# The end of the second layer: a product that sums and spreads the squares, and the power taken over 128x256 elements

## The chip, the cores and the metric

The kernel runs on one core of one Trainium2 chip. The metric is the device time of one execution in microseconds, lower is better. Engines go by their short names: PE is TensorE (PEld its weight loads), DVE is VectorE, ACT is ScalarE, POOL is GpSimd, SP is SyncE, which only issues transfers here.

## The reference

Everything is float32: the model width D is 1024, the inner width E is 2048, the sequence S is 512, and there are two layers. Only the last line below is touched by the change.

```python
def _rmsnorm(x, g):
    y = x * lax.rsqrt(jnp.mean(x * x, axis=-1, keepdims=True) + EPS)
    return y * g

for i in range(2):
    shift, scale, gate = _modulation(c, w_mod[i], b_mod[i])
    h = _rmsnorm(x, norm_g[i]) * (1.0 + scale) + shift
    y = _short_conv_mixer(h, ...) if i == 0 else _spatial_gating_mixer(h, ...)
    x = x + gate * y
return _rmsnorm(x, final_g)
```

## The kernel before

The residual `x` lies transposed in SBUF: 128 partitions hold the 128 features of one tile, KD = 8 tiles lie one behind the other (`x_b[:, k, :]`), and the 512 positions of the sequence run along the free dimension. So the mean over the features that the norm needs is a sum over the eight tiles and then over the 128 partitions, and its reciprocal root, one number for each position, must be on all partitions before it can be multiplied into `x`.

Every large product is computed in three parts (high times high, high times low, low times high) by float32r operands. In the second layer's output projection, `out_product` makes six of the eight feature tiles (three rounds of two) over all 512 positions; `last_out_product` makes the last two tiles in two halves of 256 positions (`halves[0]`, `halves[1]`), so that the norm of the first half can be made while PE computes the second.

After each pair of tiles DVE adds the gated product to `x` (`update_x`, `update_half`), ACT squares the new tiles (`square_x`, `square_half`), and DVE adds the squares into `ssum` (`add_squares`, L1446). The very last square is not added; it stays in `work[:, 1, HALF:S]` and PE adds it. For each half the order around the change is:

1. PE, `half_sums`: two products with one block of 128 columns of `ssum` as weights and one column of ones as the moving operand (L1000), and two more with the last square (L1004). The sums land with the positions on the partitions, 128x2.
2. DVE, `start_rstd` (L1450): scale and EPS, PSUM to `variance`, 128x2. It raises `var_ready`.
3. POOL (L519): `variance` to the power of -0.5 into `rstd`, all 128x4 elements. It raises `power_ready`.
4. DVE, `diagonals` (L1456): two 128x128 diagonal matrices out of the identity and `rstd`.
5. PE, `broadcast` (L1010): a matrix of ones times the diagonals, 128x256, so that every partition has the row of the 256 values.
6. DVE (L2104): for each of the 8 tiles `x = x * final_g * p_half`, reading the values from PSUM. After each two of them SP sends 128x2x256 elements out (L496).

Each engine does its instructions in the order in which they are written, and semaphores are the only order between engines. DVE's order at the end is: `update_half(1, 0)`, steps 2, 4 and 6 of the first half, then `update_half(1, 1)`, steps 2, 4 and 6 of the second. PE's order is: the two last tiles of the first half; the first round (s = 0) of the second half; `half_sums(1, 0)`; the round s = 1; `broadcast`; the rounds s = 2 and 3; then `half_sums(1, 1)`, `keep_clock(8)` (eight 128x128 products of ones, L979, whose result nobody reads) and the second `broadcast`. POOL takes six powers in all (`N_RSQRT`); numbers 5 and 6 are those of the two halves. The first layer's end and the start use the same functions and stay as they are.

Of the kernel before, what the change touches and what calls it, by code (L numbers as in the profile page):

```python
# [31 lines left out]
ALU = mybir.AluOpType  # L32

P = 128
D = 1024
S = 512
E = 2048
KD = D // P
KE = E // P
NCH = S // P  # L40
HALF = S // 2
EPS = 1e-6
# [3 lines left out]
N_RSQRT = 6  # L46
X_STEPS = KD + 2 + 1
SQUARES = KD + 2
SQ_STEPS = 1 + 6 + 2
SQ_START = 7  # L50
FREE = 2
WARM = (6, 2)
WARM_END = 8
LEAD = 0
AHEAD = 3
OFF = 6
# [81 lines left out]
def build(nc, stream, xt, cols_d, wst_d, bs_d, out):  # L138
    ctx = ExitStack()
    with ctx:  # L140
# [10 lines left out]
        def at_kb(name, kb, shape, dt=F32):  # L151
            return nc.alloc_sbuf_tensor_at(name, shape, dt, offset=base + 1024 * kb)
# [44 lines left out]
        raw = at_kb("raw", 156, [P, RING, SLOT])  # L197
        tmp = at_kb("tmp", 176, [P, 4, S])
        work = at_kb("work", 184, [P, 2, S])
        ssum = at_kb("ssum", 196, [P, S])  # L200

        cols = sb("cols", [P, N_COL])
# [3 lines left out]
        variance = sb("variance", [P, NCH])  # L206
        rstd = sb("rstd", [P, NCH])
# [4 lines left out]
        minus_half = sb("minus_half", [P, NCH])  # L212
        ones = sb("ones", [P, P])
# [30 lines left out]
        sq_ready = sem("sq_ready")  # L244
# [4 lines left out]
        sq_added = sem("sq_added")  # L249
        stat_sum, var_ready, power_ready = sem("stat_sum"), sem("var_ready"), sem("power_ready")  # L250
        half_done = sem("half_done")
        diag_ready, rstd_bc = sem("diag_ready"), sem("rstd_bc")
# [56 lines left out]
        halves = [slice(0, HALF), slice(HALF, S)]  # L309
# [45 lines left out]
        p_half = [p_rstd, p_pair[0]]  # L355
# [144 lines left out]
        @block.gpsimd  # L500
        def _(pool):
            pool.memset(ident[:, :], 0.0).then_inc(consts, 1)
            pool.memset(ones[:, :], 1.0).then_inc(consts, 1)
            pool.wait_ge(consts, 2)
            pool.affine_select(out=ident[:, :], in_=ident[:, :], compare_op=ALU.not_equal, fill=1.0, base=0,
                               pattern=[[-1, P]], channel_multiplier=1).then_inc(consts, 1)
            pool.memset(minus_half[:, :], -0.5).then_inc(consts, 1)
            pool.wait_ge(consts, 4)
            def low_b(i, g):
                pool.wait_ge(neg_b, of_b(i, g, 1, 1))  # L510
                pool.sem_inc(lo_begun_b, 1)
                pool.dma_start(wl_b[g][:, B_2:B_11].bitcast(F32), raw[:, 2 * g + 1, :],
                               accum_op=ALU.add).then_inc(b2_in_b[g], 16)

            for k in range(N_RSQRT):
                if k == 3:
                    low_b(0, 0)
                pool.wait_ge(var_ready, k + 1)
                pool.tensor_tensor(rstd[:, :], variance[:, :], minus_half[:, :], ALU.pow).then_inc(power_ready, 1)  # L519
                if k == 0:  # L520
                    for n, w in enumerate(BY_DMA):
                        slot = w_at(w)[0]
                        pool.wait_ge(neg_w, n + 1)
                        pool.dma_start(w_lo_s[:, w % 4, :].bitcast(F32), raw[:, slot, :],
                                       accum_op=ALU.add).then_inc(w_lo_in[slot], 16)
                    with pool.Fori(1, PAIRS) as i:
                        for g in range(4):
                            par = g % 2
                            pool.wait_ge(neg, of_pair(i, g, 1, 1))
                            pool.sem_inc(lo_begun, 1)  # L530
                            pool.dma_start(wl[par][:, B_2:B_11].bitcast(F32), raw[:, 2 * par + 1, :],
                                           accum_op=ALU.add).then_inc(b2_in[par], 16)
                    pool.wait_ge(y_made, PAIRS)
                if k == 3:
                    with pool.Fori(0, PAIRS - 1) as i:
                        low_b(i, 1)
                        low_b(i + 1, 0)
                    low_b(PAIRS - 1, 1)
                    pool.wait_ge(sv_used, 2 + KE)
                if k in (0, 3):  # L540
                    pool.wait_ge(stat_sum, 1 if k == 0 else 3)
                    pool.memset(ssum[:, :], 0.0).then_inc(sq_added, 1)
# [410 lines left out]
        def _(pe):  # L953
# [22 lines left out]
            def keep_clock(n):  # L976

                for _ in range(n):
                    pe.matmul(pp[3][:, 0:P], ones[:, :], ones[:, :], start=True, stop=True)  # L979
# [16 lines left out]
            def half_sums(layer, half):  # L996

                pe.wait_ge(sq_added, SQ_START + SQ_STEPS * layer + 1 + 6 + half + 1)
                for st in range(2):
                    pe.matmul(p_half[half][:, st:st + 1], ssum[:, HALF * half + P * st:HALF * half + P * (st + 1)],  # L1000
                              ones[:, 0:1], start=st == 0, stop=False, skip_group_check=True)
                pe.wait_ge(sq_ready, KD + SQUARES * layer + 6 + 2 * half + 2)
                for st in range(2):
                    mm = pe.matmul(p_half[half][:, st:st + 1], work[:, 1, HALF + P * st:HALF + P * (st + 1)],  # L1004
                                   ones[:, 0:1], start=False, stop=True, skip_group_check=True)
                mm.then_inc(stat_sum, 1)

            def broadcast(out, n, at):
                pe.wait_ge(diag_ready, n)
                pe.matmul(out, ones[:, :], work[:, 0, at], start=True, stop=True).then_inc(rstd_bc, 1)  # L1010
# [36 lines left out]
            for kp in range(4):  # L1047
# [8 lines left out]
                for n in range(2):  # L1056
                    k = 2 * kp + n
# [15 lines left out]
                for u in range(2):  # L1073
                    for n in range(2):
                        k = 2 * kp + n
                        at = slice(256 * (k % 4) + P * u, 256 * (k % 4) + P * (u + 1))
# [116 lines left out]
            def last_out_product(layer, w0):  # L1193

                for half in range(2):
                    for s in range(4):
                        out_slot(layer, w0, DPAIRS - 1, s)
                        for u in range(2):
                            if s == 0 and half == 1:
                                pe.wait_ge(x_updated, X_STEPS * layer + FREE + 6 + u)  # L1200
                            mm = unit(pp[last_bank(layer, half) + u][:, 0:HALF], weights(s, u, out_ring[layer]), rows(y_hi, halves[half]),
                                      rows(y_lo, halves[half]), range(4 * s, 4 * s + 4), s == 0, s == 3)
                            if half == 1:
                                mm.then_inc(blocks, 1)
                            elif s == 3:
                                mm.then_inc(half_done, 1)
                            if half == 1 and s == 0 and u == 1:
                                half_sums(layer, 0)
                            if half == 1 and s == 1 and u == 1:
                                broadcast(p_half[0][:, 0:HALF], 2 * layer + 3, slice(0, HALF))  # L1210


# [6 lines left out]
            for n in range(2):  # L1219
                mm = pe.matmul(p_pair[n].rearrange("q (h p) -> q h p", p=P), ones[:, :], ws[:, 4 * n:4 * n + 4, :],  # L1220
                               start=True, stop=True)
# [110 lines left out]
                out_product(1, W_BOUT, j)  # L1332
            pe.wait_ge(c_sum_b, OFF + 3 * 2 * PAIRS)
            last_out_product(1, W_BOUT)
            half_sums(1, 1)
            keep_clock(WARM_END)
            broadcast(p_half[1][:, 0:HALF], 6, slice(HALF, S))


        @block.vector  # L1340
        def _(dve):
# [5 lines left out]
            at = [0]  # L1347
# [104 lines left out]
            def diagonals(k, n, first):  # L1452

                dve.wait_ge(power_ready, k)
                for st in range(n):
                    ins = dve.tensor_scalar(work[:, 0, P * (first + st):P * (first + st + 1)], ident[:, :],  # L1456
                                            rstd[:, st:st + 1], None, ALU.mult)
                    if st < n - 1:
                        step(ins)
                ins.then_inc(diag_ready, 1)  # L1460
# [334 lines left out]
            def start_rstd(k, half):  # L1795
                dve.wait_ge(stat_sum, k if k < 4 else k - 1)
                rsqrt(k, p_half[half][:, 0:2], 1.0 / D, 2)
# [298 lines left out]

            for half in range(2):
                update_half(1, half)
                start_rstd(5 + half, half)
                diagonals(5 + half, 2, 2 * half)  # L2100
                dve.wait_ge(rstd_bc, 4 + half)
                for k in range(KD):
                    xa = x_b[:, k, halves[half]]
                    dve.scalar_tensor_tensor(out=xa, in0=xa, scalar=cols[:, C_FG + k:C_FG + k + 1],  # L2104
                                             in1=p_half[half][:, 0:HALF], op0=ALU.mult,
                                             op1=ALU.mult).then_inc(out_ready, 1)


# [74 lines left out]
```

## Time and profile before

| | us |
|---|---|
| median of 3 runs | 835.21 (833.79 to 835.49) |
| the profiled execution, its own time | 834.54 |
| its span in the trace | 832.4 |
| its mean granted PE clock | 0.994 of full speed |

The span runs from the first to the last record of the trace; the execution's own time has 2.1 us more around it. PE is busy for 97% of the span and POOL for 6%. Busy shares are those of the whole kernel; the change lies in the last 20 us, and only the records of that stretch tell what it does there. In the trace a float32 product appears as two records, so x4 is two products.

### The profile page before, as it was taken

Reading aid. Unit: us, or ns where it says so; the run is one execution under the profiler, and the core shown is the slowest. Engines: PE = TensorE matmul, PEld = TensorE weight load, DVE = VectorE, ACT = ScalarE, POOL = GpSimd, SP = SyncE. Lnnn points to the kernel's source line nnn. Section 1 sums busy time; section 2 is a strip of 40 time slices with the busy share of each in tenths; the row PEclk is TensorE's granted clock in tenths of the full one; section 3 lists DMA queues with packets and bytes.
Section 4 is the critical chain, followed back from the end, with each engine's and each line's share of the span. In section 5 each row is a group of like instructions: output and inputs, shape, how many; then the busy total and the mean of one; then the engine's idle time right before and its main releaser. Section 6 shows DMA issues by size and latency. Waiting matters only on the chain.

```text
span 832.4 us, 15163 instructions
## 1 busy us (share of the span) xinstructions
PE 804.5 (97%) x5590; PEld 750.3 (90%) x5590; DVE 643.7 (77%) x941; ACT 438.5 (53%) x617; POOL 52.1 (6%) x65
## 2 busy tenths in 40 slices
PE   5999999999999999999999999999999999899996
PEld 5779999999999999978889888899999999778896
DVE  5879999899998989887625776478888888676534
ACT  4575666666556565642225733356767666642210
POOL 1010000000100000000000000000000000000000
PEclk9999999999999999999999999999999999989999
DMA  9995565656566666497222342325445445574103
GB/s 353 364 245 140 142 201 169 208 166 189 176 184 177 197 168 198 135 378 258 96 77 77 142 162 101 101 77 152 124 128 148 135 145 151 181 299 152 51 1 102
DMA packets 39645, 138.36 MB, mean 166 GB/s; under 512 B 4288, under 2 KB 6464, under 8 KB 39616
## 3 DMA queue, kind: packets, MB, share of 16 engines
q1 hardware_dynamic: 32128, 111.16, 36.2%
q0 software_dynamic: 7056, 25.69, 16.2%
q10 hardware_dynamic: 432, 1.13, 0.3%
q8 instruction: 17, 0.28, 0.1%
q14 instruction: 12, 0.10, 0.0%
HBM read 108.09 MB, written 4.19 MB: 135 GB/s over the span
## 4 chain that ended last, share of the span: by engine, by line
PE 85%; issue 4%; ACT 4%; DVE 3%; DMA 2%; SPq 0%; POOL 0%; ACTq 0%; DVEq 0%; POOLq 0%
PE pp L1097 10%; PE pp L1098 10%; PE pp L1096 10%; PE pp L963 8%; PE pp L964 8%; PE pp L965 7%; PE p_aux L1096 6%; PE p_aux L1098 6%; PE p_aux L1097 6%; PE pp L1232 3%; PE pp L1234 3%; PE pp L1233 3%; PE pp L1053 2%; PE p_aux L1306 2%; DMA raw_s<-in_stream 1%
## 5 line engine op out<-in xcount | busy, mean ns | idle before, releaser
L1098 PE MATMUL pp<-h_hi,wl 128*128 128x256 f32 x280 | 79.2, 283 | 0.0
L1097 PE MATMUL pp<-h_lo,wh 128*128 128x256 f32 x280 | 79.2, 283 | 0.0
L1096 PE MATMUL pp<-h_hi,wh 128*128 128x256 f32 x280 | 79.2, 283 | 0.0
L1594 DVE TENSOR_TENSOR wl<-wt,wh 128x1024 fp32r<-128x1024 f32 x56 | 66.5, 1218 | 0.5 <-ACT wh L642 0.5
L642 ACT ACTIVATE wh<-wt 128x1024 fp32r<-128x1024 f32 x56 | 58.9, 1054 | 13.6 <-DVE wt L1575 7.6
L1096 PE MATMUL pp<-s_hi,wh 128*128 128x256 f32 x224 | 63.4, 283 | 0.0
L1097 PE MATMUL pp<-s_lo,wh 128*128 128x256 f32 x224 | 63.4, 283 | 0.0
L1098 PE MATMUL p_aux<-s_hi,wl 128*128 128x256 f32 x224 | 63.4, 283 | 0.0
L1098 PE MATMUL pp<-s_hi,wl 128*128 128x256 f32 x224 | 63.4, 283 | 0.0
L1097 PE MATMUL p_aux<-s_lo,wh 128*128 128x256 f32 x224 | 63.4, 283 | 0.0
L1096 PE MATMUL p_aux<-s_hi,wh 128*128 128x256 f32 x224 | 63.4, 283 | 0.0
L558 ACT ACTIVATE w_hi<-raw 128x1024 fp32r<-128x1024 f32 x29 | 30.6, 1058 | 62.0 <-PE pp L965 29.1
L963 PE MATMUL pp<-y_hi,w_hi_b 128*128 128x512 f32 (+1 forms) x160 | 57.9, 362 | 5.3 <-DVEq L2079 4.6
L963 PE MATMUL pp<-y_hi,w_hi 128*128 128x512 f32 (+1 forms) x160 | 58.5, 366 | 0.7 <-DVE y_lo L1655 0.3
L1371 DVE TENSOR_TENSOR w_lo<-raw,w_hi 128x1024 fp32r<-128x1024 f32 x32 | 38.9, 1222 | 23.1 <-ACT w_hi L558 22.4
L964 PE MATMUL pp<-y_lo,w_hi_b 128*128 128x512 f32 (+1 forms) x160 | 56.7, 354 | 0.0
L965 PE MATMUL pp<-y_hi,w_lo_b 128*128 128x512 f32 (+1 forms) x160 | 56.5, 353 | 0.0
L964 PE MATMUL pp<-y_lo,w_hi 128*128 128x512 f32 (+1 forms) x160 | 55.6, 348 | 0.0
L965 PE MATMUL pp<-y_hi,w_lo 128*128 128x512 f32 (+1 forms) x160 | 55.6, 347 | 0.0
L1097 PEld LDWEIGHTS pp<-h_lo,wh 128*128 128x128 f32 x280 | 53.8, 192 | 0.0
L1096 PEld LDWEIGHTS pp<-h_hi,wh 128*128 128x128 f32 x280 | 53.8, 192 | 0.0
L1098 PEld LDWEIGHTS pp<-h_hi,wl 128*128 128x128 f32 x280 | 53.8, 192 | 0.0
(223 smaller groups left out, 2584.2 us busy)
## 6 DMA issues: line engine op xcount, KB each, us to landing
raw<-in_stream SPq DMA_DIRECT2D x144, 512.0 KB, 4.0
wl<-raw POOLq DMA_DIRECT2D x28, 512.0 KB, 4.6
raw_l<-in_stream SPq DMA_DIRECT2D x18, 512.0 KB, 8.5
raw_s<-in_stream SPq DMA_DIRECT2D x16, 512.0 KB, 13.3
wl_b<-raw POOLq DMA_DIRECT2D x16, 512.0 KB, 4.5
raw_m<-in_stream SPq DMA_DIRECT2D x14, 512.0 KB, 3.2
w_lo_s<-raw POOLq DMA_DIRECT2D x5, 512.0 KB, 7.6
x_s<-in_xt SPq DMA_DIRECT2D x4, 512.0 KB, 5.9
```

The source lines that it names most:

```text
L558: act.activation(to[:, slot[0], :], raw[:, slot[1], :], ACT.Copy).then_inc(hi_cut, 1)
L642: act.activation(wh[g % 2][:, at], wt[g % 2][:, at], ACT.Copy).then_inc(t_hi_cut, 1)
L963: pe.matmul(out, hi, rhs_hi(kt), start=first and n == 0, stop=False)
L964: pe.matmul(out, hi, rhs_lo(kt), start=False, stop=False)
L965: mm = pe.matmul(out, lo, rhs_hi(kt), start=False, stop=last and n == len(kts) - 1)
L1096: pe.matmul(out, hi, hi_of(k), start=fresh and k == 0, stop=False, skip_group_check=not fresh)
L1097: pe.matmul(out, hi, lo_of(k), start=False, stop=False, skip_group_check=not fresh)
L1098: mm = pe.matmul(out, lo, hi_of(k), start=False, stop=k == 3, skip_group_check=not fresh)
L1232: pe.matmul(v_bank(st)[:, :], left_hi, right_hi, start=kt == 0, stop=False)
L1233: pe.matmul(v_bank(st)[:, :], left_hi, right_lo, start=False, stop=False)
L1371: dve.tensor_tensor(lo[:, slot[0], :], raw[:, slot[1], :], f32(hi[:, slot[0], :]), ALU.subtract).then_inc(consumed, 1)
L1594: dve.tensor_tensor(wl[par][:, part], wt[par][:, part], f32(wh[par][:, part]), ALU.subtract).then_inc(t_cut, 1)
```

## The change

In the second layer alone, `half_sums_wide` multiplies the matrix of ones by the 256 columns of `ssum` and then by those of the last square, into the same 128x256 block of PSUM. The sum is then on every partition at once. DVE turns it into `var_w` (128x256), POOL takes the power over 128x256 elements into `rstd_w` (the exponent is one column of `minus_half`, read 256 times), and the final multiplication reads `rstd_w` from SBUF. The diagonals, the broadcast and the eight clock keeping products are gone from this place. `var_w` and `rstd_w` lie where `work[:, 0, :]` and `tmp[:, 0, :]` are.

```diff
-WARM_END = 8
+        var_w, rstd_w = at_kb("var_w", 184, [P, S]), at_kb("rstd_w", 176, [P, S])
@@ gpsimd
                 pool.wait_ge(var_ready, k + 1)
-                pool.tensor_tensor(rstd[:, :], variance[:, :], minus_half[:, :], ALU.pow).then_inc(power_ready, 1)
+                if k < N_RSQRT - 2:
+                    pool.tensor_tensor(rstd[:, :], variance[:, :], minus_half[:, :], ALU.pow).then_inc(power_ready, 1)
+                else:
+                    at = halves[k - (N_RSQRT - 2)]
+                    pool.tensor_tensor(rstd_w[:, at], var_w[:, at], minus_half[:, 0:1].broadcast_to([P, HALF]),
+                                       ALU.pow).then_inc(power_ready, 1)
@@ tensor
+            def half_sums_wide(half):
+                out = p_half[half][:, 0:HALF]
+                pe.wait_ge(sq_added, SQ_START + SQ_STEPS + 1 + 6 + half + 1)
+                pe.matmul(out, ones[:, :], ssum[:, halves[half]], start=True, stop=False)
+                pe.wait_ge(sq_ready, KD + SQUARES + 6 + 2 * half + 2)
+                pe.matmul(out, ones[:, :], work[:, 1, HALF:S], start=False, stop=True).then_inc(stat_sum, 1)
@@ last_out_product
                             if half == 1 and s == 0 and u == 1:
-                                half_sums(layer, 0)
-                            if half == 1 and s == 1 and u == 1:
+                                if layer:
+                                    half_sums_wide(0)
+                                else:
+                                    half_sums(layer, 0)
+                            if half == 1 and s == 1 and u == 1 and not layer:
                                 broadcast(p_half[0][:, 0:HALF], 2 * layer + 3, slice(0, HALF))
@@ end of tensor
-            half_sums(1, 1)
-            keep_clock(WARM_END)
-            broadcast(p_half[1][:, 0:HALF], 6, slice(HALF, S))
+            half_sums_wide(1)
@@ end of vector
                 update_half(1, half)
-                start_rstd(5 + half, half)
-                diagonals(5 + half, 2, 2 * half)
-                dve.wait_ge(rstd_bc, 4 + half)
+                dve.wait_ge(stat_sum, 4 + half)
+                dve.tensor_scalar(var_w[:, halves[half]], p_half[half][:, 0:HALF], 1.0 / D, EPS, ALU.mult,
+                                  ALU.add).then_inc(var_ready, 1)
+                dve.wait_ge(power_ready, 5 + half)
                 for k in range(KD):
                     xa = x_b[:, k, halves[half]]
                     dve.scalar_tensor_tensor(out=xa, in0=xa, scalar=cols[:, C_FG + k:C_FG + k + 1],
-                                             in1=p_half[half][:, 0:HALF], op0=ALU.mult,
+                                             in1=rstd_w[:, halves[half]], op0=ALU.mult,
                                              op1=ALU.mult).then_inc(out_ready, 1)
```

## Rows read from the trace of the kernel before

**Rows 1.** Busy time of each engine over the whole span, share, instructions.

```profile
PE 804.5 (97%) x5590; PEld 750.3 (90%) x5590; DVE 643.7 (77%) x941; ACT 438.5 (53%) x617; POOL 52.1 (6%) x65
```

**Rows 2.** Busy time by stretch, us and instructions, the last 8.5 us.

```profile
core 0: us, PE busy (x) PEld busy (x) DVE busy (x) ACT busy (x) POOL busy (x), PEclk, DMA share, GB/s
...
823.90:832.40 8.50, 2.56 (x19) 2.00 (x18) 3.87 (x11) 0.00 (x0) 1.01 (x1) 0.78 0.37 123
```

**Rows 3.** Chain of waits in order of time, last stretch: start us, us, what.

```profile
816.88 0.12 PE pp L963
...
822.31 0.49 DVE x_b L1786
...
822.83 0.42 ACT work L783
...
823.29 0.61 PE p_aux L1004 x4
823.90 1.89 PE pp L979 x16
825.79 0.68 PE p_aux L1010 x2
...
826.49 0.48 DVE x_b L2104
```

**Rows 4.** Instructions in order of time, first half of the columns: start us, us, engine, line.

```profile
812.16 0.50 PE L1000 MATMUL p_aux<-ones,ssum 128*128 128x1 f32 x4
...
812.97 0.36 PE L963 MATMUL pp<-y_hi,w_hi_b 128*128 128x256 f32 x1
...
813.39 1.04 POOL L519 TENSOR_TENSOR rstd<-variance,minus_half 128x4 f32<-128x4 f32 x1 [88.55 <-DVE variance L1450]
...
815.93 0.59 PE L1010 MATMUL p_aux<-work,ones 128*128 128x256 f32 x2
816.17 0.47 PE L963 MATMUL pp<-y_hi,w_hi_b 128*128 128x256 f32 x1
816.48 0.28 PE L964 MATMUL pp<-y_lo,w_hi_b 128*128 128x256 f32 x1
...
816.56 3.22 DVE L2104 SCALAR_TENSOR_TENSOR x_b<-x_b,cols,p_aux 128x256 f32<-128x256 f32 x8 [1.61 <-PE p_aux L1010]
```

**Rows 5.** Instructions in order of time, second half of the columns.

```profile
820.87 0.48 DVE L1786 SCALAR_TENSOR_TENSOR x_b<-pp,mod,x_b 128x256 f32<-128x256 f32 x1 [1.09 <-PE pp L965]
...
824.18 1.01 POOL L519 TENSOR_TENSOR rstd<-variance,minus_half 128x4 f32<-128x4 f32 x1 [9.75 <-DVE variance L1450]
```

**Rows 6.** Two powers of layer one and the vector engine beside them.

```profile
443.81 1.04 POOL L519 TENSOR_TENSOR rstd<-variance,minus_half 128x4 f32<-128x4 f32 x1 [86.37 <-DVE variance L1450]
...
443.92 1.23 DVE L1371 TENSOR_TENSOR w_lo<-raw,w_hi 128x1024 fp32r<-128x1024 f32 x1 [0.20 <-ACT w_hi L558]
...
459.06 1.21 DVE L1371 TENSOR_TENSOR w_lo<-raw,w_hi 128x1024 fp32r<-128x1024 f32 x1
...
459.22 1.92 POOL L519 TENSOR_TENSOR rstd<-variance,minus_half 128x4 f32<-128x4 f32 x1 [14.37 <-DVE variance L1450]
```

**Rows 7.** GpSimd's other instructions, its groups by line, then in order of time.

```profile
L542 POOL MEMSET ssum<- 128x512 f32 x2 | 1.1, 528 | 29.8 <-DVE y L1649 15.5 <-DVE work L2005 14.3
...
0.89 0.21 POOL L503 MEMSET ones<- 128x128 f32 x1
1.34 0.29 POOL L505 TENSOR_SCALAR_AFFINE_SELECT ident<-ident 128x128 f32<-128x128 f32 x1 [0.25 <-POOL ones L503]
1.58 0.10 POOL L507 MEMSET minus_half<- 128x4 f32 x1
```

**Rows 8.** Groups of vector instructions by line and shape: busy us, mean ns.

```profile
L1422 DVE SCALAR_TENSOR_TENSOR acc_b<-raw_l,silu_c,acc_b 128x256 f32<-128x256 f32 x42 | 20.4, 485 | 1.9
...
L1943 DVE TENSOR_TENSOR tmp<-pp,pc_b 128x256 f32<-128x256 f32 x16 | 6.7, 417 | 1.3 <-PE pp L1098 1.3
...
L2104 DVE SCALAR_TENSOR_TENSOR x_b<-x_b,cols,p_aux 128x256 f32<-128x256 f32 x16 | 6.4, 475 | 2.4 <-PE p_aux L1010 2.4
```

## The prediction, made before the changed kernel ran

> **What bounds the kernel now.** I read the busy shares first: PE works 97% of the span and POOL 6% [rows 1]. That says that no time is won by relieving POOL in general, but nothing of the end, since the change touches only the last 20 us. So the second view is the stretch from 823.90 us on: of 8.50 us PE is busy 2.56, DVE 3.87 and POOL 1.01 [rows 2]. No engine is full there; the end is a chain of short steps, each of which waits for the one ahead. The third view, the chain of waits, gives these steps in order [rows 3]: DVE adds the last tile (822.31), ACT squares it (822.83 to 823.25), PE sums (823.29 to 823.90), then the eight clock keeping products and the broadcast, and DVE begins to multiply at 826.49. In the chain 823.90 to 825.79 is booked on L979, but that is only what PE did meanwhile: the broadcast had to wait for POOL's power, 824.18 to 825.19 [rows 5], and for the diagonals behind it. From 826.49 to the end of the span at 832.4 are 5.91 us, which hold eight multiplications and the last transfer, and the change leaves them in kind.
>
> For the first half of the columns the same steps lie beside PE's products [rows 4]: DVE's eight multiplications run 816.56 to 819.78, and DVE then sits idle 1.09 us until PE frees it at 820.87 [rows 5]. That idle time is all the slack that the first half has.
>
> **The change part by part.**
>
> PE, first half. The narrow sums stop the stream from 812.16 to 812.97, 0.81 us [rows 4]. For the wide form the nearest row is the broadcast, a product of the same shape: the stream's products begin 0.12 us apart [rows 3], at the broadcast it is 815.93, 816.17, 816.48, so it costs 0.24 + 0.31 - 0.12 = 0.43 us [rows 4]. Two wide products cost 0.86, and the broadcast's 0.43 goes: PE gets to its last product 0.81 + 0.43 - 0.86 = 0.38 us earlier. If DVE is free, its last update then begins at 820.49 instead of 820.87.
>
> DVE. The 128x256 evacuation from PSUM replaces one of 128x2. The nearest row is L1943, 128x256 out of PSUM, 417 ns [rows 8]; I take 0.40 us. The diagonals go. The multiplications read their second operand from SBUF instead of PSUM: with all operands in SBUF L1422 takes 485 ns, with PSUM L2104 takes 475 [rows 8]. Eight times 10 ns is 0.08 at most, taken as nothing.
>
> POOL. This is the term that decides, and no row shows a power over more than four columns. Call its duration T. The record for 128x4 is 1.01 to 1.04 us [rows 4, 5], and it is not the price of a first call: the one at 824.18 is the next instruction that POOL computes after the one at 813.39, and is only 0.03 shorter. What is inside this microsecond? Two records tell. At 443.81 a large DVE instruction starts 0.11 us after the power and doesn't disturb it, 1.04 us. At 459.06 the same DVE instruction starts 0.16 us ahead of it, and the power takes 1.92: it ends at 461.14, which is 0.87 us after DVE's end at 460.27 [rows 6]. So POOL reads all its operands in about the first 0.1 us and is held when DVE is reading; the other 0.87 us is computing and writing of four columns. Against that, a memset of the same 128x4 is 0.10 us, one of 128x128 0.21 and one of 128x512 0.53 [rows 7]: moving a column costs (528 - 206) / 384 = 0.84 ns. The microsecond is therefore the power's own arithmetic, and the question is how much of it comes again with each column.
>
> Lower bound: none of it does, and each further column costs what a memset's does, T = 1.03 + 252 x 0.00084 = 1.24 us. Upper bound: all but the memset's 0.10 is proportional, T = 0.10 + 256 x 0.93 / 4 = 59.6 us. I take a value near the upper end, since the only row of a power is nearer to it: a fixed part of 0.34 us, the memset's 0.10 and the 0.24 that lies between the end of a memset's record (0.89 + 0.21) and the instruction that waits for it at 1.34 [rows 7], and 0.69 / 4 = 0.1725 us a column. T = 0.34 + 256 x 0.1725 = 44.5 us.
>
> A rule of the Trainium skill gives this a reason. GPSIMD Engine Reference, Performance pitfalls for Q7 kernels: a dependent chain of float32 operations costs 4 cycles for each of them unless independent work fills in. At the 1.2 GHz of its Specifications, 0.1725 us is 207 cycles, as an estimate some 52 dependent operations for a column. No row here shows whether columns overlap.
>
> The sum. First half: the wide sums end at 812.16 + 0.43 + 0.59 = 813.18; DVE takes 0.05 + 0.40; POOL starts 0.08 later, ends after T; DVE multiplies 0.04 behind it, at 813.75 + T, for 3.22 us. DVE is free at 817.0 + T. Its next instruction is the last half's update; behind it wait ACT's squares, PE's sums, the second power and everything to the end. So the update begins at U, the later of 820.49 and 817.0 + T. Up to T = 3.5 the first power is hidden by PE's products, and beyond that each microsecond of T counts twice. Second half: from the update to the last square 2.38 us, as before (820.87 to 823.25 [rows 3, 5]); wide product with the last square 0.04 + 0.66 (the record of the broadcast is 0.59 and 0.68 [rows 3, 4]); evacuation 0.04 + 0.40; T with 0.08 and 0.04 around it; then the 5.91 us. The span is U + 9.55 + T. The keep-clock products go and cost nothing: they lay beside the power, and nothing of PE is left behind it.
>
> With T = 44.5, U = 861.5 and PE has stood idle for some 40 us. In the last stretch, with PE idle at its end, the granted clock averages 0.78 [rows 2]; so PE's wide product then runs at the lower level, 1.2 of 2.4 GHz, at most twice as long, and I add 0.4. The span is 861.5 + 9.55 + 44.5 + 0.4 = 915.95, against 832.4: 83.6 us more. On the profiled execution's 834.54 this is 918.1; the median of the runs is 0.67 above that, so I predict **918.8 us**.
>
> **Rivals.**
>
> *Flat power.* The microsecond is the latency of one pass and the columns stream behind it, T = 1.24. Then the first half is hidden and the span is 820.49 + 9.55 + 1.24 = 831.28, 1.1 us less: 834.1 us. From the last square to the multiplication, the before needs 3.24 us (823.25 to 826.49), the after 1.26 + T, so up to T = 1.98 that path alone pays, and with PE's 0.38 the break-even is at T = 2.36, or 5.3 ns for each added column. For it speaks that the same engine moves a column in 0.84 ns; against it, that the power spends 0.87 us without reading. Even so it can't win 0.2% (1.67 us): that would need T below 0.7, less than the four columns take now. So in this case the measurement sees no change.
>
> GPSIMD Engine Reference, Elementwise side-by-side, counts 2.6 cycles for an element of a two-input add, 0.55 us for 256 columns. If the power kept that pace T would be 1.58 and the time 834.4, as an estimate; an add isn't a power, and rows 6 and 7 speak against it.
>
> *Partly overlapped.* The power's columns share a loop that overlaps several of them: 10 to 60 ns a column, T from 3.6 to 16, the span 2T - 5.9 + 0.4 us longer once T passes 3.5. At 25 ns T = 7.3, +9.1 us, 844 us; at 60 ns T = 16.2, +27, 862 us. For it: rows 6 allow any split of the 0.87 into a first column and the rest.
>
> *Fully proportional.* T = 59.6: 2 x 59.6 - 5.45 = +113.8 us, 949 us. It is the upper end of my own case.
>
> **How the numbers follow.** A column at over 60 ns, my case: 0.56. Partly overlapped: 0.26. Flat, under 10 ns: 0.18. About 0.2% of 835 us, 1.67 us, is what the measurement tells from no change. Of the flat case 0.15 is within it and 0.03 faster; both others are slower, 0.82. My own case alone runs from 862 to 952 us. The range is 835 to 952: it takes in the partly overlapped case and a piece of the flat one, and leaves out most of the flat one and what lies above proportional.
>
> **What would show each step.** The two records of POOL's power in the last stretch: their duration is T, and T - 1.03 over 252 is the price of a column. The last L1786 pair of DVE should begin 817 + T (or at 820.5 if T is under 3.5), with POOL as what ended DVE's idle time. PE's product stream should have one stop of about 0.86 us and no second one, and be done 0.4 us earlier. The evacuation should be 0.40 us, the eight multiplications 3.2 us, and the granted clock low from PE's last product on. If a power of 256 columns takes under 3.5 us, the prediction is wrong by its main term and the time is within 1 or 2 us of before; if it takes 10 us, it is wrong in size only.

## The result, and the profile after

The changed kernel takes 911.73 us (median of 4 runs, 910.13 to 912.20) against 835.35 before (4 runs, 833.79 to 835.72). The ratio is 1.0918, 95% interval 1.0899 to 1.0937: 9.2% slower, +76.4 us. The prediction was 918.8 us. The profiled execution took 912.20 us with a span of 910.1.

Groups of instructions after, from the page of the profile (line, engine, operation, out<-in, count, then busy us and mean ns, and idle time ahead). The first row is the power, which now heads the list; in the kernel before the page did not list it:

```profile
L523 POOL TENSOR_TENSOR rstd_w<-var_w,minus_half 128x256 f32<-128x256 f32 x2 | 82.3, 41138 | 94.8 <-DVE var_w L2114 94.8
...
L2119 DVE SCALAR_TENSOR_TENSOR x_b<-x_b,cols,rstd_w 128x256 f32<-128x256 f32 x16 | 6.5, 479 | 82.5 <-POOL rstd_w L523 82.5
```

GpSimd's records in order of time, kernel after (start us, us, engine, line, operation, and in brackets the idle time ahead and what ended it). They answer to [rows 4, 5]: 1.04 and 1.01 us there, 41.16 and 41.12 here.

```profile
814.55 41.16 POOL L523 TENSOR_TENSOR rstd_w<-var_w,minus_half 128x256 f32<-128x256 f32 x1 [87.58 <-DVE var_w L2114]
862.98 41.12 POOL L523 TENSOR_TENSOR rstd_w<-var_w,minus_half 128x256 f32<-128x256 f32 x1 [7.27 <-DVE var_w L2114]
```

The same for DVE. It does nothing for 41.28 us in the first half of the columns and for 41.23 in the second, and both times it is the power that ends the idle time. Between the two, from 855.75 to 862.89, lie the multiplications, the update and the second evacuation:

```profile
814.04 0.42 DVE L2114 TENSOR_SCALAR var_w<-p_aux 128x256 f32<-128x256 f32 x1 [3.26 <-PE p_aux L1019]
855.75 3.26 DVE L2119 SCALAR_TENSOR_TENSOR x_b<-x_b,cols,rstd_w 128x256 f32<-128x256 f32 x8 [41.28 <-POOL rstd_w L523]
858.92 0.48 DVE L1800 SCALAR_TENSOR_TENSOR x_b<-pp,mod,x_b 128x256 f32<-128x256 f32 x1
...
862.47 0.42 DVE L2114 TENSOR_SCALAR var_w<-p_aux 128x256 f32<-128x256 f32 x1 [1.77 <-PE p_aux L1019]
904.13 3.25 DVE L2119 SCALAR_TENSOR_TENSOR x_b<-x_b,cols,rstd_w 128x256 f32<-128x256 f32 x8 [41.23 <-POOL rstd_w L523]
```

PE in order of time, kernel after. The stop in the stream is two wide products; L969 begins at 813.96 where it would have at 813.10 (0.12 us behind 812.98), so they cost 0.86 us as taken, and there is no second stop. The last stream product begins at 822.34, which is 9.36 us after the first sum; before, it was 9.83 (821.99 - 812.16), so PE is done 0.47 us earlier and not 0.38. Then PE does nothing until 860.36, and the same two products then take longer:

```profile
812.98 0.59 PE L1017 MATMUL p_aux<-ssum,ones 128*128 128x256 f32 x2
813.41 0.59 PE L1019 MATMUL p_aux<-work,ones 128*128 128x256 f32 x2
813.65 0.47 PE L968 MATMUL pp<-y_hi,w_hi_b 128*128 128x256 f32 x1
813.96 0.28 PE L969 MATMUL pp<-y_lo,w_hi_b 128*128 128x256 f32 x1
...
822.34 0.28 PE L970 MATMUL pp<-y_hi,w_lo_b 128*128 128x256 f32 x1
860.36 1.22 PE L1017 MATMUL p_aux<-ssum,ones 128*128 128x256 f32 x2 [37.74 <-DVE ssum L1460]
861.37 1.06 PE L1019 MATMUL p_aux<-work,ones 128*128 128x256 f32 x2
```

The chain of waits, kernel after, its longest pieces. It reads 41.16 us of power, 7.23 of what lies between, 41.16 of power. The 7.23 us are booked as "issue" and the second power on POOL's queue (POOLq); it is DVE's and PE's records above that tell what happened between the powers. Before, the same view had L1004, L979 and L1010 here [rows 3].

```profile
814.55 41.16 POOL rstd_w L523
855.71 7.23 issue
862.94 41.16 POOLq L139
```

**One measure for all kernels.** Runs differ by some microseconds in when they reach the output projection, so I compare kernels by one distance inside the trace: from the first sum of squares on PE in the first half to the first multiplication of the second half. Before it is 826.49 - 812.16 = 14.33 us [rows 3, 4]; after it is 904.13 - 812.98 = 91.15, which is +76.82. What follows the second start is alike (5.91 us before, 5.97 after).

### The profile page after: what moved, and what is told of

Its sections match the earlier page's. It is cut to its first block, busy times and chain, and to the rows that moved or that the text cites. A ratio compares the mean times of both kernels' runs of the same rounds, so it can differ in the third digit from the quotient of the medians.

```text
span 910.1 us, 15103 instructions
## 1 busy us (share of the span) xinstructions
PE 804.7 (88%) x5562; PEld 750.6 (82%) x5562; DVE 643.4 (71%) x937; ACT 438.3 (48%) x617; POOL 132.2 (15%) x65
## 4 chain that ended last, share of the span: by engine, by line
PE 76%; issue 5%; POOL 5%; POOLq 5%; DVE 4%; ACT 3%; DMA 1%; SPq 0%; ACTq 0%; DVEq 0%
PE pp L1110 9%; PE pp L1111 9%; PE pp L1109 9%; PE pp L968 7%; PE pp L969 7%; PE pp L970 6%; PE p_aux L1109 6%; PE p_aux L1111 6%; PE p_aux L1110 6%; POOLq L139 5%; POOL rstd_w L523 5%; PE pp L1248 2%; PE pp L1249 2%; PE pp L1250 2%; PE p_aux L1322 2%
## 5 line engine op out<-in xcount | busy, mean ns | idle before, releaser
L523 POOL TENSOR_TENSOR rstd_w<-var_w,minus_half 128x256 f32<-128x256 f32 x2 | 82.3, 41138 | 94.8 <-DVE var_w L2114 94.8
L2119 DVE SCALAR_TENSOR_TENSOR x_b<-x_b,cols,rstd_w 128x256 f32<-128x256 f32 x16 | 6.5, 479 | 82.5 <-POOL rstd_w L523 82.5
L536 POOL DMA_DIRECT2D wl<-raw x28 | 24.1, 862 | 266.4 <-ACT wl L639 266.4
L969 PE MATMUL pp<-y_lo,w_hi_b 128*128 128x512 f32 (+1 forms) x160 | 56.1, 351 | 0.0
L969 PE MATMUL pp<-y_lo,w_hi 128*128 128x512 f32 (+1 forms) x160 | 55.6, 348 | 0.0
```

Of the source, the lines that this page charges most:

```text
L523: pool.tensor_tensor(rstd_w[:, at], var_w[:, at], minus_half[:, 0:1].broadcast_to([P, HALF]), ALU.pow).then_inc(power_ready, 1)
L969: pe.matmul(out, hi, rhs_lo(kt), start=False, stop=False)
```

## The experiments

**sweep: what a power costs by its width.** On the kernel before, GpSimd gets thirteen more instructions in its idle stretch, into scratch space:

```diff
+                if k == 3:
+                    pool.memset(probe_in[:, :], 3.7).then_inc(probe, 1)
+                    done = 1
+                    for base, parts, n, op in ([(probe_in, P, n, ALU.pow) for n in (1, 2, 4, 8, 16, 32, 64, 128)]
+                                               + [(ones, P, 4, ALU.pow), (ones, P, 64, ALU.pow),
+                                                  (probe_in, 16, 64, ALU.pow), (probe_in, P, 128, ALU.mult),
+                                                  (probe_in, P, HALF, ALU.mult)]):
+                        pool.wait_ge(probe, done)
+                        pool.tensor_tensor(probe_out[0:parts, 0:n], base[0:parts, 0:n],
+                                           minus_half[0:parts, 0:1].broadcast_to([parts, n]), op).then_inc(probe, 1)
+                        done += 1
```

> The kernel before, with thirteen extra instructions on GpSimd in its idle stretch between 725 and 813 us, whose results nobody reads: powers of 1 to 128 columns of one value, two powers of another value, one on 16 partitions, and two products of 128 and 256 columns in their place. Theory (each column costs its own arithmetic): from 1.03 us at 4 columns and 41.14 us at 256 a column is 40.1 / 252 = 0.159 us and the fixed part 0.39, so 0.55, 0.71, 1.03, 1.66, 2.9, 5.5, 10.6 and 20.8 us for 1 to 128 columns; 64 columns on 16 partitions also 10.6; the other value the same; the products under 1 us. Rival (the cost comes with the large instruction or with the exponent that is read again and again, not with the power): the products of 128 and 256 columns, which read the same exponent column, take tens of us too. The kernel's time stays at 835 us by both, since the whole row ends some 65 us after 725.

Measured: 834.11 us in one run (before 835.37, median of 3). GpSimd's groups by shape, kernel sweep (busy us, mean ns; the row of 128x128 holds the power, 20.73 us, and the product):

```profile
L554 POOL TENSOR_TENSOR probe_out<-probe_in,minus_half 128x128 f32<-128x128 f32 x2 | 21.5, 10728 | 0.2
...
L554 POOL TENSOR_TENSOR probe_out<-probe_in,minus_half 16x64 f32<-16x64 f32 x1 | 10.6, 10624 | 0.1
L554 POOL TENSOR_TENSOR probe_out<-probe_in,minus_half 128x64 f32<-128x64 f32 x1 | 10.5, 10522 | 0.1
L554 POOL TENSOR_TENSOR probe_out<-ones,minus_half 128x64 f32<-128x64 f32 x1 | 10.5, 10520 | 0.1
...
L554 POOL TENSOR_TENSOR probe_out<-probe_in,minus_half 128x32 f32<-128x32 f32 x1 | 5.9, 5868 | 0.1
...
L554 POOL TENSOR_TENSOR probe_out<-probe_in,minus_half 128x4 f32<-128x4 f32 x1 | 1.0, 1007 | 0.1
...
L554 POOL TENSOR_TENSOR probe_out<-probe_in,minus_half 128x2 f32<-128x2 f32 x1 | 0.7, 703 | 0.1
L554 POOL TENSOR_TENSOR probe_out<-probe_in,minus_half 128x256 f32<-128x256 f32 x1 | 0.6, 613 | 0.1
```

The last row is the product of 256 columns. From 64 to 128 columns the power grows by 10.21 us, 0.16 us a column; from 2 to 4 by 0.304, 0.152 a column. With the 41.14 us of 256 columns in the changed kernel, the widths 2, 4, 64, 128 and 256 lie on one line, 0.39 us and 0.159 a column, to within 0.05 us. The value makes no difference (3.7 or 1.0, 10.52 us each for 64 columns), and 16 partitions cost what 128 do (10.62). The product reads the same repeated exponent and takes 0.61 us for 256 columns, 67 times less than the power, so the rival falls: the price belongs to the power, not to the size or the repeated operand. The widths 1, 8, 16 and 32 lie above the line by up to 0.6 us (5.87 for 32, where it gives 5.48); each of these four began while DVE ran an instruction with two operands in SBUF, which the last section takes up. The power of 2 columns began at the same 725.95 us as a DVE instruction with one operand in PSUM and one in SBUF, and took its 0.70.

**wide_first and wide_second: where the price is paid.** In wide_first the second half goes by `half_sums`, the power of 128x4, diagonals and broadcast as before; in wide_second the first half does. The excerpt leaves out DVE's part, which follows the same choice: per half either the evacuation and the wait for the wide power, or `start_rstd`, `diagonals` and the broadcast.

```diff
 wide_first
-                if k < N_RSQRT - 2:
+                if k != N_RSQRT - 2:
-            half_sums_wide(1)
+            half_sums(1, 1)
+            keep_clock(8)
+            broadcast(p_half[1][:, 0:HALF], 5, slice(HALF, S))
 wide_second
-                if k < N_RSQRT - 2:
+                if k != N_RSQRT - 1:
 (last_out_product: half_sums and broadcast for both layers, as before)
```

> The wide form in the first half of the columns alone, the second half as before. Theory: DVE waits for the power until 855, multiplies, and begins the last update at 817.0 + 41.1 = 858.1 instead of 820.9, +37.3; PE has idled by then and its eight clock keeping products, now at the lower clock, take about 3.8 instead of 1.9 us and are longer than power and diagonals together, so +1.9, and sums and broadcast at the lower clock +0.8: +40.0, 875 us. Rival (the first half lies beside PE's products and is hidden, the second pays for all): within 1 us of 835.

> The wide form in the second half alone, the first as before. Theory: from the last square to the multiplication 1.26 + 41.14 us instead of 3.24, +39.2, 874.5 us; PE has not idled before, so nothing for its clock. Rival (the second pays for all): +76 us, 912. With wide_first the two add up to about 79 us, 2 to 3 more than both together (76.4), because in the changed kernel the clock keeping products are gone.

Measured: wide_first 873.88 us (2 runs), ratio 1.0465 (1.0434 to 1.0495); wide_second 874.07 (2 runs), ratio 1.0467 (1.0428 to 1.0506). By the distance inside the trace wide_first is 865.19 - 811.75 = 53.44, +39.11; wide_second 866.95 - 813.41 = 53.54, +39.21, as expected, and not the +76 of a second half that pays for all. Instructions in order of time, kernel wide_first:

```profile
857.69 0.48 DVE L1802 SCALAR_TENSOR_TENSOR x_b<-pp,mod,x_b 128x256 f32<-128x256 f32 x1
...
860.86 3.76 PE L984 MATMUL pp<-ones 128*128 128x128 f32 x16
...
861.28 1.01 POOL L520 TENSOR_TENSOR rstd<-variance,minus_half 128x4 f32<-128x4 f32 x1 [6.79 <-DVE variance L1466]
862.32 0.48 DVE L1472 TENSOR_SCALAR work<-ident,rstd 128x128 f32<-128x128 f32 x2 [1.12 <-POOL rstd L520]
864.41 0.74 PE L1023 MATMUL p_aux<-work,ones 128*128 128x256 f32 x2
865.19 3.22 DVE L2126 SCALAR_TENSOR_TENSOR x_b<-x_b,cols,p_aux 128x256 f32<-128x256 f32 x8 [2.39 <-PE p_aux L1023]
```

The last update and the multiplications behind it, kernel wide_second:

```profile
822.12 0.48 DVE L1797 SCALAR_TENSOR_TENSOR x_b<-pp,mod,x_b 128x256 f32<-128x256 f32 x1 [1.09 <-PE pp L970]
...
866.95 3.26 DVE L2121 SCALAR_TENSOR_TENSOR x_b<-x_b,cols,rstd_w 128x256 f32<-128x256 f32 x8 [41.24 <-POOL rstd_w L523]
```

The last update begins 45.94 us after the first sum (857.69 - 811.75) instead of 8.71, +37.2, as worked out: of the first power all but the slack of PE's rounds is paid. So the rival of a hidden first half falls. The clock keeping products take 3.76 us instead of the 2.03 at the full clock (two_columns, below), and the broadcast starts 1.61 us after the diagonals are done at 862.80. It was expected at the lower clock too, but takes 0.74, near the 0.70 of the full clock and not the 1.06 of the changed kernel; that is 0.3 of the 0.9 by which +40.0 was too high. The two kernels add up to +78.3, 1.5 more than both changes together (+76.8). The 1.5 is the difference between what PE's idling costs the narrow and the wide form of the second half, from update to multiplication. The narrow one takes 7.50 us in wide_first against 5.62 before, so 1.88, of which 1.61 is the wait behind the clock keeping products. The wide one takes 45.21 in the changed kernel against 44.83 in wide_second, so 0.38.

**update_first: why the two powers are 7.2 us apart.**

```diff
             for half in range(2):
                 update_half(1, half)
                 dve.wait_ge(stat_sum, 4 + half)
                 dve.tensor_scalar(var_w[:, halves[half]], p_half[half][:, 0:HALF], 1.0 / D, EPS, ALU.mult,
                                   ALU.add).then_inc(var_ready, 1)
+            for half in range(2):
                 dve.wait_ge(power_ready, 5 + half)
                 for k in range(KD):
```

> The changed kernel with DVE's order alone altered: the last half's update and evacuation stand ahead of the wait for the first power. Theory (GpSimd's two powers are the chain, and the 7.2 us between them are the multiplications and the update queued behind DVE's wait): the second power begins when the first ends, at 855.8, so 7.2 us less than the changed kernel, 904.5 us. Rival (the two powers overlap across GpSimd's cores, or the second is slowed by the multiplications that now run beside it, two SBUF inputs each): some other number, up to 41 us less or 3 us more than that.

Measured: 907.64 us (2 runs, 906.10 and 909.18), ratio to before 1.0869 (1.0818 to 1.0920). That is 4.1 less than the changed kernel's median and 3.1 more than the 904.5 expected. The two runs are 3 us apart, so the saving is read from the trace: 896.70 - 812.84 = 83.86 us, 7.29 less than the changed kernel's 91.15. Instructions in order of time, kernel update_first (x2 with 82.25 us are both powers, one behind the other):

```profile
814.41 82.25 POOL L523 TENSOR_TENSOR rstd_w<-var_w,minus_half 128x256 f32<-128x256 f32 x2 [87.62 <-DVE var_w L2114]
...
823.51 0.70 PE L1019 MATMUL p_aux<-work,ones 128*128 128x256 f32 x2 [0.27 <-ACT work L788]
824.24 0.42 DVE L2114 TENSOR_SCALAR var_w<-p_aux 128x256 f32<-128x256 f32 x1 [1.24 <-PE p_aux L1019]
855.60 3.61 DVE L2120 SCALAR_TENSOR_TENSOR x_b<-x_b,cols,rstd_w 128x256 f32<-128x256 f32 x8 [30.94 <-POOL rstd_w L523]
```

The powers do not overlap (82.25 is twice 41.12), and the 7.2 us were the work that DVE had queued behind its wait. The second power is not slowed by the multiplications beside it either; it is the first of these that is slowed, 0.84 us instead of 0.48 (the last section has the records). It also prices the clock: here PE's second pair of sums comes right after its stream and the last one takes 0.70 us, where the changed kernel needed 1.06 after 38 us of idling.

**mult: the change without its power.**

```diff
-                                       ALU.pow).then_inc(power_ready, 1)
+                                       ALU.mult).then_inc(power_ready, 1)
```

> The changed kernel with the power on GpSimd replaced by a product of the same operands and shape, so the norm's root is not computed. Everything else of the change stands alone then. Theory (only the power's duration is at fault; the rest is worth 2.36 us less that duration): the product takes about 0.6 us, so 1.8 us less than before, 833.5 us. Rival (the wide products, the evacuation of 128x256 and the missing clock keeping cost something too): at or above 835 us.

Measured: 832.93 us (12 runs; before 834.35, 29 runs), ratio 0.9988 (0.9969 to 1.0007), which alone tells nothing from no change. Inside the trace it is 824.92 - 812.36 = 12.56 us, 1.77 less than before, as expected. Instructions in order of time, kernel mult:

```profile
824.27 0.61 POOL L523 TENSOR_TENSOR rstd_w<-var_w,minus_half 128x256 f32<-128x256 f32 x1 [9.73 <-DVE var_w L2114]
824.92 3.25 DVE L2119 SCALAR_TENSOR_TENSOR x_b<-x_b,cols,rstd_w 128x256 f32<-128x256 f32 x8 [0.73 <-POOL rstd_w L523]
```

So nothing else of the change costs time by itself. The whole loss comes with the power: its duration, and what waits for it, PE's lower clock included. In parts the saving is 0.46 us up to the last update (it begins 8.25 us after the first sum instead of 8.71, expected 0.38 less) and 1.31 behind it (4.31 us instead of 5.62, expected 1.37 less).

**two_columns: the narrow power, narrower.** The kernel before, with the power of each half over the two columns that it needs:

```diff
-                pool.tensor_tensor(rstd[:, :], variance[:, :], minus_half[:, :], ALU.pow).then_inc(power_ready, 1)
+                n = NCH if k in (0, 3) else 2
+                pool.tensor_tensor(rstd[:, 0:n], variance[:, 0:n], minus_half[:, 0:n], ALU.pow).then_inc(power_ready, 1)
```

> The kernel before, with the power taken over the 2 columns that a half needs instead of all 4. Theory (0.159 us a column): 0.71 instead of 1.03 us, 0.3 us off the chain of the second half; but the eight clock keeping products take 1.89 us and variance, power and diagonals then 1.6, so PE is not free sooner and the broadcast starts at most 0.1 us earlier: within 0.2 us of before. Rival (a fixed microsecond): 1.03 us still.

Measured: 835.30 us (12 runs; before 834.35), ratio 1.0006 (0.9988 to 1.0025), no difference. The power takes 0.69 to 0.71 us, so the rival of a fixed microsecond falls. The distance is 831.21 - 817.10 = 14.11, 0.22 less than before, a little more than the 0.1 expected: the diagonals are done at 830.33 and the broadcast, behind the clock keeping products, begins at 830.57. In the kernel before the diagonals were done at 825.70 and the broadcast began at 825.76, so there it waited for the power's chain, as the prediction reads it, but by little more than 0.1 us. Instructions in order of time, kernel two_columns:

```profile
828.71 2.03 PE L980 MATMUL pp<-ones 128*128 128x128 f32 x16
...
829.12 0.69 POOL L520 TENSOR_TENSOR rstd<-variance,minus_half 128x2 f32<-128x2 f32 x1 [10.07 <-DVE variance L1451]
829.85 0.48 DVE L1457 TENSOR_SCALAR work<-ident,rstd 128x128 f32<-128x128 f32 x2 [0.81 <-POOL rstd L520]
830.57 0.60 PE L1011 MATMUL p_aux<-work,ones 128*128 128x256 f32 x2
```

**act_rsqrt: the wide product with the root on ACT.** A version to beat both: the spread sum stays, and ACT reads it from PSUM and writes the reciprocal root. The excerpt leaves out the memset of `eps` and what goes: GpSimd's two wide powers and DVE's evacuation.

```diff
+        eps = sb("eps", [P, 1])
@@ scalar
-            square_half(1, 0)
-            square_half(1, 1)
+            for half in range(2):
+                square_half(1, half)
+                act.wait_ge(stat_sum, 4 + half)
+                act.activation(rstd_w[:, halves[half]], p_half[half][:, 0:HALF], ACT.Abs_reciprocal_sqrt, bias=eps[:, 0:1],
+                               scale=1.0 / D).then_inc(power_ready, 1)
```

> The wide product, with the reciprocal root taken by ACT (Abs_reciprocal_sqrt, scale 1/1024, bias EPS) straight from PSUM into rstd_w, so no evacuation by DVE and nothing on GpSimd. Theory (what the change removes is worth having once the root is cheap): 0.04 + 0.66 + 0.04 + 0.40 + 0.04 = 1.18 us from the last square to the multiplication instead of 3.24, and PE 0.38 earlier: 2.4 us less than before, 832.9 us. Rival (ACT has to load another table for this function, on the path of each half): at or above before.

Measured: 832.87 us (12 runs) against 834.35 (29 runs), ratio 0.9974 (0.9955 to 0.9992). Inside the trace 823.58 - 811.67 = 11.91 us, 2.42 less than before. ACT's instructions in order of time, kernel act_rsqrt:

```profile
809.94 1.28 ACT L953 ACT_TABLE_LOAD   x1
812.73 0.48 ACT L953 ACTIVATE rstd_w<-p_aux,eps 128x256 f32<-128x256 f32 x1 [1.51 <-PE p_aux L1019]
820.43 0.42 ACT L785 ACTIVATE work<-x_b 128x256 f32<-128x256 f32 x1 [7.23 <-DVE x_b L1800]
821.87 0.42 ACT L785 ACTIVATE work<-x_b 128x256 f32<-128x256 f32 x1 [1.02 <-DVE x_b L1800]
823.07 0.47 ACT L953 ACTIVATE rstd_w<-p_aux,eps 128x256 f32<-128x256 f32 x1 [0.79 <-PE p_aux L1019]
```

The table is loaded once, at 809.94, while ACT waits for the first sum anyway, and the squares of the second half do not force it out. So the rival of a reload on the path falls. The upper end of the interval, 0.9992, lies just under 1: a small gain, barely clear of no change.

## Why the prediction was right

*The power.* The one term that decided was T, and no row showed it. It was taken as 44.5 us and measured 41.14: the price of a column was put at 0.1725 us and is 0.159, the fixed part at 0.34 and is 0.39 (1.03 - 4 x 0.159). The bounds were 1.24 and 59.6. That it came so near is partly luck. The two records of [rows 6] part reading from the rest, but, as the prediction says, they allow any split of the 0.87 us into a first column and further ones, so no row decided between the line near the upper end and the partly overlapped one; that was a chance of 0.56 against 0.26. The fixed part came from a memset's 0.10 and a gap of 0.24 between two records [rows 7], and that gap is a wait outside any record, with no known bearing on the inside of a power; the 0.34 happened to lie near the measured 0.39. The range was wide enough for both cases, and it is the sweep that shows the mechanism, a price for each column. The flat rival fell with the first record of 41.16 us, the partly overlapped one with it (at most 16 us), and the fully proportional one by its size. The 4-cycle rule of the Trainium skill (GPSIMD Engine Reference, Performance pitfalls for Q7 kernels) would make 0.159 us, as an estimate, some 48 dependent operations; no run shows what the operations are, only that each further column adds the same time. The 2.6 cycles that the Trainium skill counts for an element of a two-input add (GPSIMD Engine Reference, Elementwise — side-by-side cycle accounting) give, as an estimate, 0.55 us for 256 columns, and the product's record is 0.61: near for a product, and no guide to the power.

*The sum.* Put the measured T into it and it gives 2 x 41.14 - 5.45 = +76.83 us; the trace says +76.82. The parts stand as well: evacuation 0.42 (taken 0.40), update at 858.92 after a first sum at 812.98, so 45.94 us (taken 4.84 + T = 45.98), from there to the second evacuation 3.55 us (taken 3.52, with the 0.4 for the clock). That the last agrees to 0.03 hides two misses that cancel: the last square was done 2.24 us after the update (taken 2.38), and evacuation began 1.31 us behind it (taken 1.14), because the second wide product also had to wait for the first, slow one. The granted clock was 0.50 there, the level of 1.2 GHz. Stretch view of the kernel after: length, then PE, PEld, DVE, ACT and POOL busy with their counts, granted clock, DMA share, GB/s:

```profile
857.00:862.00 5.00, 1.64 (x4) 1.01 (x4) 3.22 (x9) 0.83 (x2) 0.00 (x0) 0.50 0.63 210
```

*Twice, less the slack.* wide_first showed that the first half's power is paid but for what lies beside PE's rounds, and wide_second that the second's is paid in full. *The gain in the flat case* was put at 2.36 us less T; mult (T = 0.61, expected -1.75, measured -1.77) and act_rsqrt (expected -2.4, measured -2.42) confirm it, and with it the break-even near 2.36 us (2.38 by mult). Here too two misses of under 0.1 us cancel. The stop of the narrow sums was taken as 0.81 us, from 812.16 to 812.97, but by the way in which the broadcast was counted it is 0.89: the next product begins 0.20 us behind 812.97 and not 0.12. So PE gains 0.46 and not 0.38. Against that, from the last square to the multiplication mult needs 1.94 us (1.87 by the sum) and act_rsqrt 1.29 (1.18). PE in order of time, kernel before:

```profile
813.17 0.28 PE L964 MATMUL pp<-y_lo,w_hi_b 128*128 128x256 f32 x1
```

*What was off.* The 918.8 us is 7.1 too high, and 6.7 of that is twice the 3.36 us by which T was over-sized. I had set the fixed part 0.05 us too small; each column then carried 0.0135 us too much, 256 times and twice.

## What to carry to other kernels

When an operation moves to a shape with more elements on each partition, what matters is how its price splits into a fixed part and one for each column, and the trace may show it only at one width: bound it by a cheap operation of the same engine, and test the width alone before building on it. Spreading a value over the partitions before an expensive function multiplies that function's columns (2 to 256 here), so the order "function, then spread" is worth a product and two diagonals unless the function runs at the pace of a copy. A wait that an in-order engine makes for a late result also delays all that is queued behind it; here the two powers would have stood in a row in any case (update_first), and the wait put 7.2 us of other work between them.

## What the runs showed of the hardware

- A power on GpSimd costs 0.39 us and 0.159 us a column, at 2, 4, 64, 128 and 256 columns, whatever the value (3.7 or 1.0) and whether 16 or 128 partitions take part; a product of two operands takes 0.61 us for 256 columns.
- A power's reads are held while DVE runs an instruction with two operands in SBUF, and the rest of its time follows after that. In the kernel sweep a power of four columns began at 771.00, beside such an instruction that ran from 770.30 to 771.53, and ended at 772.40: 0.87 us after it, the same 0.87 as in [rows 6]. That fits its 1.40 us instead of 1.01. This DVE instruction, which had begun first, was not slowed, 1.23 us:

```profile
770.30 1.23 DVE L1385 TENSOR_TENSOR w_lo_b<-raw,w_hi_b 128x1024 fp32r<-128x1024 f32 x1 [3.46 <-ACT w_hi_b L572]
771.00 1.40 POOL L554 TENSOR_TENSOR probe_out<-ones,minus_half 128x4 f32<-128x4 f32 x1
```

- It goes the other way when the power begins first. In update_first the second power began 0.04 us ahead of the first multiplication, which has two operands in SBUF too: the power took 41.10 us as ever, the multiplication 0.84 instead of 0.48, and the seven behind it their usual time. So by this record a power of 256 columns holds DVE for some 0.4 us and not for its whole 41:

```profile
855.56 41.10 POOL L523 TENSOR_TENSOR rstd_w<-var_w,minus_half 128x256 f32<-128x256 f32 x1
855.60 0.84 DVE L2120 SCALAR_TENSOR_TENSOR x_b<-x_b,cols,rstd_w 128x256 f32<-128x256 f32 x1 [30.94 <-POOL rstd_w L523]
```

- In the changed kernel PE's last stream product begins at 822.34; its granted clock was 1.00 from 822.6 to 826 us and 0.50 from 830 on, so it was low long before PE had work again at 860.36, and a float32 product of 128x256 then took 1.06 instead of 0.70 us. In wide_first PE worked from 859.13 on without a stop, at 0.50 through the two sums and the eight products of 128x128 (3.76 us); over the broadcast behind them the clock averaged 0.80, and the broadcast took 0.74. Stretch view of wide_first, columns as above:

```profile
864.40:865.15 0.75, 0.75 (x4) 0.35 (x2) 0.00 (x0) 0.00 (x0) 0.00 (x0) 0.80 0.00 0
```
